# A decoder step on one Trainium2 core: gathers of selected cache rows on 128 partitions, and a reordered combining stage

## What is computed

```python
_, idx = lax.top_k(score, min(N_SEL, n_sel))
gathered = jax.vmap(jax.vmap(lambda blocks, ix: blocks[ix]))(sel_blocks, idx.transpose(0, 2, 1, 3))
...
o_s = jnp.einsum('btgqnk,bgtnkd->btgqd', p_s.astype(gathered.dtype), gathered[..., 1, :])
```

```python
y = yb[dest] * sw[:, None].astype(yb.dtype)
return jax.ops.segment_sum(y, tok, num_segments=T)
...
xp = xp + ga2p * f[:n_p].reshape(xp.shape)
xs = xs + ga2s * f[n_p:].reshape(xs.shape)
y_prompt = rms_norm(xp, final_g)
```

## Time and profile before

| | |
|---|---|
| median of 3 runs | 2125.15 us (2122.95 to 2130.14) |
| the profiled execution's own time | 2130.52 us |
| its span, first to last instruction | 2128.7 us |
| mean granted TensorE clock | 0.944 of full speed |
| PE / DVE / ACT / POOL busy | 89% / 60% / 50% / 11% of the span |
| data moved by DMA | 443.21 MB, mean 208 GB/s |

### The profile page before, as it was taken

How to read it: one execution, slowest core, us unless ns; L and a number is a source line. 1 busy time by engine, 2 the same in 40 slices (tenths; PEclk the granted TensorE clock), 3 DMA queues, 4 the chain that set the end, 5 groups by cost and what they waited for, 6 DMA issues and landing times. The chain is left out here.

```text
span 2128.7 us, 27808 instructions
## 1 busy us (share of the span) xinstructions
PE 1897.4 (89%) x9998; PEld 1481.8 (70%) x9998; DVE 1287.5 (60%) x1988; ACT 1074.0 (50%) x1684; POOL 224.0 (11%) x203
## 2 busy tenths in 40 slices
PE   6899995999998899888776799689999999999946
PEld 2699775999995567777332355478888888888832
DVE  1533523444434456777432466589999888887826
ACT  5312112444424667777321221078888888886722
POOL 0100000000001222333110000011000000000011
PEclk9899997999996999999998899789999999999977
DMA  8320125743214337022093822189999999999836
GB/s 291 89 99 33 50 80 202 245 181 128 88 43 141 128 107 215 14 85 50 17 217 74 317 104 99 53 316 426 427 424 413 415 414 413 413 416 356 344 144 255
DMA packets 155368, 443.21 MB, mean 208 GB/s; under 512 B 37322, under 2 KB 82318, under 8 KB 123570
## 3 DMA queue, kind: packets, MB, share of 16 engines
q1 hardware_dynamic: 136292, 341.10, 43.1%
q0 software_dynamic: 13792, 81.90, 11.4%
q10 hardware_dynamic: 5184, 18.88, 2.2%
HBM read 387.34 MB, written 58.70 MB: 210 GB/s over the span
## 5 line engine op out<-in xcount | busy, mean ns | idle before, releaser
L2824 DVE TENSOR_TENSOR moe_lo<-wts_raw,moe_hi 128x2048 fp32r<-128x2048 f32 x216 | 484.8, 2287 | 74.5 <-ACT moe_hi L2721 73.9
L2721 ACT ACTIVATE moe_hi<-wts_raw 128x2048 fp32r<-128x2048 f32 x216 | 402.4, 1915 | 54.0 <-PE moe_U L2602 24.4
L949 DVE TENSOR_TENSOR cmp_xl<-cmp_bank,cmp_xh 128x512 fp32r<-128x512 f32 (+1 forms) x136 | 82.6, 668 | 120.0 <-ACT cmp_xh L903 119.9
L1419 POOL TENSOR_SCALAR att_prow<-att_prow,att_scale 128x640 f32<-128x640 f32 (+15 forms) x96 | 113.4, 1194 | 370.1 <-DVE att_scale L1554 370.1
L873 PE MATMUL cmp_hp<-cmp_xh,cmp_wh 128*128 128x256 f32 (+2 forms) x512 | 150.5, 294 | 0.0
L873 PE MATMUL cmp_hp<-cmp_xh,cmp_wl 128*128 128x256 f32 (+2 forms) x512 | 146.7, 287 | 0.0
L873 PE MATMUL cmp_hp<-cmp_xl,cmp_wh 128*128 128x256 f32 (+2 forms) x512 | 146.3, 286 | 0.0
L1527 DVE TENSOR_TENSOR att_pl<-att_pT,att_ph 128x512 fp32r<-128x512 f32 (+5 forms) x148 | 101.2, 688 | 72.2 <-ACT att_ph L1453 71.8
L2022 POOL DMA_INDIRECT rou_xg<-s_h,rou_idx x36 | 49.5, 1375 | 803.8 <-PE moe_XT L2607 512.6
L1463 ACT ACTIVATE att_prow<-att_S,att_low 128x640 f32<-128x640 f32 (+15 forms) x192 | 107.5, 560 | 41.2 <-DVE att_low L1542 37.7
L2628 PE MATMUL moe_Y<-moe_hi,moe_hh 128*128 128x512 f32 x288 | 114.4, 397 | 10.9 <-DVE moe_hl L2844 7.9
(11 more groups left out here) (451 smaller groups left out, 4364.9 us busy)
## 6 DMA issues: line engine op xcount, KB each, us to landing
wts_raw<-in_w_gate SPq DMA_DIRECT2D x72, 1024.0 KB, 7.1
wts_raw<-in_w_up SPq DMA_DIRECT2D x72, 1024.0 KB, 7.7
wts_raw<-in_w_down SPq DMA_DIRECT2D x72, 1024.0 KB, 8.6
s_yb<-moe_y ACTq DMA_DIRECT2D x36, 512.0 KB, 7.9
smi_kvs<-in_w_ada SPq DMA_DIRECT2D x8, 2048.0 KB, 8.3
fro_wraw<-in_w_ada SPq DMA_DIRECT2D x4, 2048.0 KB, 11.4
s_yb<-att_zero SPq DMA_DIRECT2D x1, 8192.0 KB, 32.7
fro_wraw<-in_w_in SPq DMA_DIRECT2D x12, 512.0 KB, 5.4
```

Source lines behind the costliest of these rows:

```text
L1419: last = pool.tensor_scalar(row, row, scale[:, grp, h:h + 1], None, ALU.mult)
L2721: act.activation(hi[p][half][:, :], raw[p][half][:, :], ACT.Copy).then_inc(hi_ready[p], 1)
L2824: dve.tensor_tensor(lo[p][half][:, :], raw[p][half][:, :], hi[p][half][:, :], ALU.subtract).then_inc(lo_ready[p], 1)
```

## The change

It has two parts. In sample attention the indirect DMA writes all 128 partitions and takes all 128 indices of its column; nothing else there changes, and rows 120 to 127 are not read.

In combine the tiles are taken in the order `seq`: the sample tile first, then prompt tiles 0 to 7. Every engine counts positions i in that order, so position 0 is the sample tile and positions 1 to 8 are prompt tiles. SP first loads the two modulation rows, then the residual rows; from position 4 on each residual load is followed by the store of the position four before; the last four positions are stored after the loop. There are four output buffers, each with its semaphore. The final gain has a semaphore of its own, for which DVE waits before the first `norm`. The stage takes the identity that the routing stage has already in SBUF, and loads none.

```diff
@@ sample attention, POOL
-                pool.indirect_dma_start(kv[u % NKV][0:SP, :, :].rearrange("p t c -> p (t c)"), None, rows,
-                                        bass.IndirectOffsetOnAxis(ap=idx[0:SP, u:u + 1], axis=0)
+                pool.indirect_dma_start(kv[u % NKV][:, :, :].rearrange("p t c -> p (t c)"), None, rows,
+                                        bass.IndirectOffsetOnAxis(ap=idx[:, u:u + 1], axis=0)
...
@@ combine
-        out = [s.sb(f"out{i}", [P, D]) for i in range(2)]
-        ident = s.sb("ident", [P, P])
+        NOUT = 4
+        LATE = 4
+        out = [s.sb(f"out{i}", [P, D]) for i in range(NOUT)]
+        ident = rt.ident
...
+        seq = [TT - 1] + list(range(TT - 1))
+
+        def store(sp, i):
+            t = seq[i]
             n = rows_of(t)
-            sp.wait_ge(normed, t + 1)
+            sp.wait_ge(normed, i + 1)
             dst = a["o_y_p"][0, t * P:t * P + n, :] if t < NT else a["o_y_s"][:, 0, :]
-            sp.dma_start(dst, out[t % 2][0:n, :]).then_inc(out_done[t % 2], 16)
+            sp.dma_start(dst, out[i % NOUT][0:n, :]).then_inc(out_done[i % NOUT], 16)
 
         @block.sync
         def _(sp):
-            sp.dma_start(ident[:, :], a["c_ident"]).then_inc(ident_in, 16)
-            for t in range(TT):
+            sp.dma_start(mods[:, :], a["s_mod"][0:NB, 5 * D:6 * D]).then_inc(const_in, 16)
+            sp.dma_start(mod[:, :], a["s_mod"][NB:NB + 1, 5 * D:6 * D].to_broadcast([P, D])).then_inc(const_in, 16)
+            for i, t in enumerate(seq):
                 n = rows_of(t)
-                if t:
-                    sp.wait_ge(y_in[t - 1], 32)
-                sp.dma_start(x2[t][0:n, :], a["s_x2"][t * P:t * P + n, :]).then_inc(x_in[t], 16)
-                if t == 0:
-                    sp.dma_start(mod[:, :], a["s_mod"][NB:NB + 1, 5 * D:6 * D].to_broadcast([P, D])).then_inc(const_in, 16)
-                    sp.dma_start(mods[:, :], a["s_mod"][0:NB, 5 * D:6 * D]).then_inc(const_in, 16)
-                    sp.dma_start(gf[:, :], a["final_g"].to_broadcast([P, D])).then_inc(const_in, 16)
-            for t in range(TT):
-                store(sp, t)
-            sp.wait_ge(out_done[0], 16 * ((TT + 1) // 2))
-            sp.wait_ge(out_done[1], 16 * (TT // 2))
+                if i:
+                    sp.wait_ge(y_in[i - 1], 32)
+                sp.dma_start(x2[i][0:n, :], a["s_x2"][t * P:t * P + n, :]).then_inc(x_in[i], 16)
+                if i == 0:
+                    sp.dma_start(gf[:, :], a["final_g"].to_broadcast([P, D])).then_inc(gain_in, 16)
+                if i >= LATE:
+                    store(sp, i - LATE)
+            for i in range(TT - LATE, TT):
+                store(sp, i)
+            for k in range(NOUT):
+                sp.wait_ge(out_done[k], 16 * len(range(k, TT, NOUT)))
 
         @block.gpsimd
         def _(pool):
-            for t in range(TT):
+            for i, t in enumerate(seq):
                 n = rows_of(t)
                 for k, dst in enumerate((y1, y2)):
-                    pool.indirect_dma_start(dst[t][0:n, :], None, a["s_yb"],
+                    pool.indirect_dma_start(dst[i][0:n, :], None, a["s_yb"],
                                             bass.IndirectOffsetOnAxis(ap=slot[0:n, k, t:t + 1], axis=0)
-                                            ).then_inc(y_in[t], 16)
+                                            ).then_inc(y_in[i], 16)
...
-            def norm(t):
-                n = rows_of(t)
-                dve.wait_ge(root, t + 1)
-                if t >= 2:
-                    dve.wait_ge(out_done[t % 2], 16 * (t // 2))
...
+            def norm(i):
+                n = rows_of(seq[i])
+                dve.wait_ge(root, i + 1)
+                if i == 0:
+                    dve.wait_ge(gain_in, 16)
+                if i >= NOUT:
+                    dve.wait_ge(out_done[i % NOUT], 16 * (i // NOUT))
...
```

More of the change, by code:

```diff
@@ L3055, in stage_combine @@
         y_in = [s.sem(f"y_in{i}") for i in range(TT)]
-        ident_in = s.sem("ident_in")
         diag_ready = s.sem("diag_ready")
@@ L3064, in stage_combine @@
         vch = s.sem("vch")
-        out_done = [s.sem(f"out_done{i}") for i in range(2)]
+        out_done = [s.sem(f"out_done{i}") for i in range(NOUT)]
+        gain_in = s.sem("gain_in")
         block = s.block()
-        def store(sp, t):
+        seq = [TT - 1] + list(range(TT - 1))
+        def store(sp, i):
+            t = seq[i]
             n = rows_of(t)
-            sp.wait_ge(normed, t + 1)
+            sp.wait_ge(normed, i + 1)
             dst = a["o_y_p"][0, t * P:t * P + n, :] if t < NT else a["o_y_s"][:, 0, :]
-            sp.dma_start(dst, out[t % 2][0:n, :]).then_inc(out_done[t % 2], 16)
+            sp.dma_start(dst, out[i % NOUT][0:n, :]).then_inc(out_done[i % NOUT], 16)
@@ L3105, in _ @@
             act.wait_ge(wgt_ready, 1)
-            act.wait_ge(ident_in, 16)
-            for t in range(TT):
+            for i, t in enumerate(seq):
                 n = rows_of(t)
                 for k in range(2):
-                    last = act.activation(diag[0:n, t, k, 0:n], ident[0:n, 0:n], ACT.Copy, scale=rt.wgt[0:n, k, t:t + 1])
+                    last = act.activation(diag[0:n, i, k, 0:n], ident[0:n, 0:n], ACT.Copy, scale=rt.wgt[0:n, k, t:t + 1])
                 last.then_inc(diag_ready, 1)
-            for t in range(TT):
+            for i, t in enumerate(seq):
                 n = rows_of(t)
[L3114 to L3117, removed]
+                act.wait_ge(summed, i + 1)
+                act.activation(junk[0:n, :], x2[i][0:n, :], ACT.Square, accum_out=stat[0:n, i, 0:1]).then_inc(ss, 1)
+                act.wait_ge(ss, i + 1)
+                act.activation(stat[0:n, i, 1:2], stat[0:n, i, 0:1], ACT.Sqrt, bias=eps[0:n, :], scale=1.0 / D
                                ).then_inc(root, 1)
@@ L3121, in _ @@
         def _(pe):
-            for t in range(TT):
+            for i, t in enumerate(seq):
                 n = rows_of(t)
[L3124 to L3127, removed]
+                pe.wait_ge(diag_ready, i + 1)
+                pe.wait_ge(y_in[i], 32)
+                if i >= 4:
+                    pe.wait_ge(gated, i - 3)
                 for k, y in enumerate((y1, y2)):
                     for c in range(2):
-                        last = pe.matmul(F[t % 4][c][0:n, :], diag[0:n, t, k, 0:n], y[t][0:n, c * 512:(c + 1) * 512],
+                        last = pe.matmul(F[i % 4][c][0:n, :], diag[0:n, i, k, 0:n], y[i][0:n, c * 512:(c + 1) * 512],
                                          start=(k == 0), stop=(k == 1))
@@ L3147, in _, with add @@
             dve.wait_ge(wgt_ready, 1)
-            dve.wait_ge(const_in, 48)
-            def add(t):
+            dve.wait_ge(const_in, 32)
+            def add(i):
+                t = seq[i]
                 n = rows_of(t)
                 m = (mod if t < NT else mods)[0:n, :]
-                f, x = f1[t % 2][0:n, :], x2[t][0:n, :]
-                dve.wait_ge(mixed, t + 1)
+                f, x = f1[i % 2][0:n, :], x2[i][0:n, :]
+                dve.wait_ge(mixed, i + 1)
                 for c in range(2):
                     cs = slice(c * 512, (c + 1) * 512)
-                    last = dve.tensor_tensor(f[:, cs], F[t % 4][c][0:n, :], m[:, cs], ALU.mult)
+                    last = dve.tensor_tensor(f[:, cs], F[i % 4][c][0:n, :], m[:, cs], ALU.mult)
                 last.then_inc(gated, 1)
-                dve.wait_ge(gated, t + 1)
-                dve.wait_ge(x_in[t], 16)
+                dve.wait_ge(gated, i + 1)
+                dve.wait_ge(x_in[i], 16)
                 dve.tensor_tensor(x, x, f, ALU.add).then_inc(summed, 1)
-            def norm(t):
-                n = rows_of(t)
-                dve.wait_ge(root, t + 1)
-                if t >= 2:
-                    dve.wait_ge(out_done[t % 2], 16 * (t // 2))
-                step(dve.reciprocal(stat[0:n, t, 2:3], stat[0:n, t, 1:2]))
-                dve.scalar_tensor_tensor(out=out[t % 2][0:n, :], in0=x2[t][0:n, :], scalar=stat[0:n, t, 2:3],
+            def norm(i):
[5 more added lines that the diff above has]
+                    dve.wait_ge(out_done[i % NOUT], 16 * (i // NOUT))
+                step(dve.reciprocal(stat[0:n, i, 2:3], stat[0:n, i, 1:2]))
+                dve.scalar_tensor_tensor(out=out[i % NOUT][0:n, :], in0=x2[i][0:n, :], scalar=stat[0:n, i, 2:3],
                                          in1=gf[0:n, :], op0=ALU.mult, op1=ALU.mult).then_inc(normed, 1)
```

## The result

The changed kernel takes 2099.65 us in the median of 4 runs (2097.65 to 2102.05), the one before 2125.02 (2122.95 to 2130.14). The ratio is 0.9878 with a 95% interval of 0.9857 to 0.9898, so it is 25.4 us or 1.2% faster. Forecast were 2095.8 in a range of 2088 to 2106.

A forecast was written before the change was run, and what follows sets the result against it. Gathers at 215 GB/s were taken to bound sample attention, and a full DMA, then DVE, to bound combine. Gains of 18.3 + 11.1 = 29.4 us off the median 2125.15 gave 2095.8 us, range 2088 to 2106.

The forecast's parts named there:

- The gathers' rate: Sample attention: 128-row gathers run at 433 GB/s instead of 215, 2.4 us of transfer each, landing in 6.1 us.
- The first rival: Sample attention: gathers stay at 215 GB/s, unit 11 comes 3.7 us later; total 2117.8 us, chance 0.07.
- the third: Sample attention: full-width gathers are slower than 120-row ones, at 150 GB/s 29 us more; total 2143 us, chance 0.03.
- TensorE as the next bound: Sample attention: TensorE bounds at 2.70 us a unit, unit 15 starts at 1124.1 instead of 1142.36, 18.3 us less.
- all that follows waits for this unit: Sample attention after unit 15: second half's softmax and values, barrier and next stage all move with its 18.3 us.
- Combine: Last stage: reordered tiles and early stores end it at 2117.6 against 2128.7, 11.1 us less, bounds 4.7 to 13.
- TensorE takes 5.06 us for it and I allow one more for a colder start: Combine, sample tile first: landed by 2068.8, TensorE has finished it at 2074.9.
- Tile 0's landing: Combine: the sample tile's gathers delay it by 0 to 2.5 us; half taken, 2073.5 instead of 2072.3.
- It waits for TensorE: Combine, last tile: DVE is ready for its add by 2105.6 but TensorE finishes only at 2108.5.
- The three early stores: Combine: positions 1 to 3 add 1.57 MB to a full DMA, delaying the last tile's gathers by 3.9 us.
- The tail: Combine: from the last tile's add to the last instruction stays 9.1 us.
- The second rival: Combine: reads and writes together slow the DMA, last landing 6.4 us later, gain 4.7 us; total 2102.2 us, chance 0.08.

The follow-up runs named there:

- the run with the gathers alone: The kernel before with 128-row gathers and combine as before: 2111.2 us against 2126.19, ratio 0.9925.
- the run with the unused products: The changed kernel with five unused 128 x 512 products on TensorE at the start of combine: combine 54.3 us, whole kernel 2097.67 us against 2124.56.

## Why the prediction was right, and where its steps were off

**The gathers' rate: right.** 433 GB/s taken, 417 measured; landings of 6.1 us worked out, 6.2 the median. The first rival (215 GB/s, 2117.8 us) and the third (slower, 2143) are out, and the run with the gathers alone shows 15.0 us for them in the total, 17.1 by unit 15 (82.6 to 65.5).

**TensorE as the next bound: right, and by a little, as worked out.** Unit 15 was worked out for 64.4 us after the first gather (1124.1 less 1059.75) and came at 64.0, so 18.6 us earlier than before. Of these, 17.5 reached the stage's end. The step "all that follows waits for this unit" took the tail as fixed, but its turn and values ran longer, 1.00 and 9.48 us where before they took 0.65 and 8.75. Both follow a wait of 3.6 us in both kernels, and in the runs here the second half's values take 8.75 to 10.12 us. The granted clock goes with it: 0.50 from 1129 to 1135 in the changed kernel, 0.50 only from 1152 to 1154 in the one before. It is no effect of the change, since the run with the gathers alone had 8.75 again.

**Combine: the gain right in size by luck, one term mis-sized, the last bound named wrongly.** 11.1 us forecast, 9.7 measured.
- The step "TensorE takes 5.06 us for it and I allow one more for a colder start" failed. The sample tile took 7.1 us and the full tile behind it 5.6 in place of 3.67, at a granted clock of 0.50 and then 0.67. The 5.06 us came from a row that began with the clock still up (1.00 from 2105.6 to 2107.6, then 0.50). TensorE also began the sample tile 0.7 us later than worked out, 7.8 us after SP's first issue. DVE got its first full tile at 20.4 us, not at 2078.6 - 2061.7 = 16.9. In the run with the unused products it came at 16.3, so the cold start is worth 4.2 us.
- Tile 0's landing was delayed by nothing: the load that waits for it went out 2048.66 - 2038.48 = 10.2 us after SP's first issue, before 10.6; I had taken 1.2 us more.
- "It waits for TensorE" at the last tile failed: DVE had no wait there. TensorE's last tile ended at 2082.93, 3.0 us before DVE came to it. The three early stores did not bound the end; DVE's own 3.85 us a tile did, from its late start. Two errors cancelled: TensorE was done with the last tile 2.4 us sooner than forecast (44.4 us against 46.8), and DVE came to it 3.5 us later (47.4 against 43.9). So the last `add`, put at 46.8 us, came at 47.4.
- The tail is 9.9 us and not 9.1: the last tile is now a full one, and its store is 0.524 MB.

**The second rival** (loads and stores pull each other down, a gain of 4.7 us) is out. SP's new waits held a load back until the norm had ended, as the pairs of store and load 0.4 us apart show, and it cost DVE nothing.

**The sum.** 29.4 forecast; 27.2 by the stages; 25.4 by the medians, with the difference between the latter two inside the scatter.

## What to carry to other kernels

When the DMA share is 1 and the rate is half of what other stages reach, look at the partitions that the transfer covers before its size: here 8 rows more in each gather, 7% more bytes that nobody reads, nearly doubled its rate. The rule is measured here for gathers of 8 KB rows alone, and why it holds is open. After that the question is what stands next in line, and its price can be read from stretches of the same trace that the old bound did not touch. A small tile put first to fill a wait runs on a cold TensorE and can hand its delay on to the tile behind it; take its price from a row that starts cold.

## What I had not expected of the hardware

Gathers of 8 KB rows moved 210, 249, 268, 212 and 417 GB/s for 64, 96, 112, 120 and 128 partitions with the queue full: not monotone, and far off full rate for every count short of 128. And while TensorE worked on a tile of 8 x 8 weights for 7 us without a break, the granted clock stayed at 0.50. The full tile behind it then had 4 us more at 0.52 (2053.4 to 2057.4) before the clock rose, as a full tile of the kernel before had that started from an idle TensorE (0.50 from 2072.4 to 2076.4) and finished in 6.0 us (2072.41 to DVE's start at 2078.45). In these rows the small tile did nothing to bring the clock up.
